# Last three projection tiles and part of the first row tile's projection placed among the first 45 attention units; sample transfers reordered

## The reference

```
z = h @ w_in                                   # q, k, v are the last three blocks of 256 columns
q, k = rms(q, q_norm) * 64**-0.5, rms(k, k_norm)
for win, dil in ((128,1), (512,4), (2048,16)): # prompt: blocks of 128 queries, 256 keys;
    s = q @ k.T + bias; m = max(s); p = exp(s - m); o = p @ v / sum(p)   # samples: + 2048 cached rows
attn = softmax-weighted merge of the patterns' outputs
mix = concat(out_a, out_b, out_c, attn), each of the four normalized
x  = x + g1 * (mix @ w_out)
h2 = rms(x) * (1 + sc2) + sh2
x  = x + g2 * moe(h2)                          # 4 groups x 8 experts, two per token
```

## Time and profile before

| | us |
|---|---|
| median of 3 runs | 2401.43 |
| the runs | 2401.43, 2389.86, 2404.76 |
| profiled execution | 2399.02 |
| its span, first to last instruction | 2397.3 |
| PE busy / DVE / ACT / POOL | 2175.1 / 853.0 / 562.8 / 284.5 |
| mean granted clock | 0.944 |
| DMA | 438.91 MB, mean 183 GB/s |

### The profile page before, as it was taken

How to read it: one execution, slowest core, us unless ns; L and a number is a source line. 1 busy time by engine, 2 the same in 40 slices (tenths; PEclk the granted TensorE clock), 3 DMA queues, 4 the chain that set the end, 5 groups by cost and what they waited for, 6 DMA issues and landing times.

```text
span 2397.3 us, 27992 instructions
## 1 busy us (share of the span) xinstructions
PE 2175.1 (91%) x7615; PEld 1094.5 (46%) x7616; DVE 853.0 (36%) x1969; ACT 562.8 (23%) x1110; POOL 284.5 (12%) x463
## 2 busy tenths in 40 slices
PE   4999999999797999999598199999999999999895
PEld 1344455545454755656234144444444444444342
DVE  3566464026562455564464511111111111111112
ACT  3410010235532434443122111111111111111111
POOL 0001020100000000001131211111111111111111
PEclk8999999999898589999899599999999999999998
DMA  9253132433447522234754545765479788787873
GB/s 377 94 215 84 31 84 51 158 105 97 126 142 204 174 76 100 87 107 152 237 204 177 190 148 161 269 229 157 162 271 344 261 325 299 238 287 290 293 248 71
DMA packets 122756, 438.91 MB, mean 183 GB/s; under 512 B 31955, under 2 KB 70579, under 8 KB 102115
## 3 DMA queue, kind: packets, MB, share of 16 engines
q1 hardware_dynamic: 92520, 309.99, 35.3%
q0 software_dynamic: 26032, 112.64, 17.2%
q10 hardware_dynamic: 4112, 15.14, 1.6%
HBM read 356.39 MB, written 83.10 MB: 183 GB/s over the span
## 4 chain that ended last, share of the span: by engine, by line
PE 81%; DVE 6%; DMA 5%; issue 3%; ACT 2%; POOL 1%; SPq 1%; DVEq 0%; ACTq 0%; POOLq 0%
PE bank L2550 20%; PE bank L2191 15%; PE bank L2578 10%; PE bank L2455 7%; PE bank L2554 4%; PE bank L2299 3%; PE bank L2354 3%; PE bank L2331 2%; PE bank L2581 2%; PE bank L2516 2%; PE bank L2341 2%; PE bank L2303 1%; PE bank L2271 1%; DMA arena<-xT 1%; DMA arena<-kc 1%
## 5 line engine op out<-in xcount | busy, mean ns | idle before, releaser
L2550 PE MATMUL bank<-arena 128*128 128x512 f32 x1120 | 492.8, 596 | 14.7 <-issue 14.7
L2191 PE MATMUL bank<-arena 128*128 128x512 f32 (+1 forms) x960 | 358.2, 533 | 9.6 <-ACTq L1066 9.6
L2550 PEld LDWEIGHTS bank<-arena 128*128 128x128 f32 x1120 | 212.6, 191 | 290.9 <-issue 290.9
L2578 PE MATMUL bank<-arena 128*128 128x512 f32 x560 | 249.6, 598 | 12.8 <-issue 12.6
L2191 PEld LDWEIGHTS bank<-arena 128*128 128x128 f32 x960 | 168.0, 191 | 193.6 <-issue 192.8
L2455 PE MATMUL bank<-arena 128*128 128x512 f32 x512 | 245.8, 604 | 0.0
L2083 DVE COPY arena<-bank 128x512 f32<-128x512 f32 x50 | 34.7, 693 | 552.0 <-PE bank L2565 552.0
L2578 PEld LDWEIGHTS bank<-arena 128*128 128x128 f32 x560 | 103.0, 189 | 136.5 <-issue 128.7
L2093 DVE TENSOR_TENSOR arena<-bank,arena 128x512 f32<-128x512 f32 (+1 forms) x50 | 34.5, 691 | 257.0 <-PE bank L2578 212.1
L2455 PEld LDWEIGHTS bank<-arena 128*128 128x128 f32 x512 | 88.6, 192 | 77.1 <-issue 77.0
L985 POOL DMA_INDIRECT o_y<-arena x50 | 79.3, 1585 | 310.5 <-issue 172.8
(11 more groups left out here) (475 smaller groups left out, 2564.6 us busy)
## 6 DMA issues: line engine op xcount, KB each, us to landing
arena<-wg SPq DMA_DIRECT2D x32, 2048.0 KB, 12.1
arena<-wu SPq DMA_DIRECT2D x32, 2048.0 KB, 16.9
arena<-wd SPq DMA_DIRECT2D x32, 2048.0 KB, 8.1
arena<-mod_w SPq DMA_DIRECT2D x12, 2048.0 KB, 18.2
z_d<-arena ACTq DMA_DIRECT2D x12, 1056.0 KB, 6.5
arena<-z_d POOLq DMA_DIRECT2D x10, 1056.0 KB, 7.7
arena<-kc POOLq DMA_DIRECT2D x8, 1280.0 KB, 10.6
arena<-vc POOLq DMA_DIRECT2D x8, 1280.0 KB, 8.2
```

The source lines that it names most:

```text
L2191: ins = mm(bank[n % 2][:, 0:w], wz[:, i % 3, k, :], hT[:, k, t0:t0 + w], start=(k == 0), stop=(k == KT - 1))
L2550: ins = mm(bank[bk][:, :], xgT[:, s, k, :], m[w][:, k, :], start=(k == 0), stop=(k == KT - 1))
L2578: ins = mm(bank[4 + h][:, :], hhT[:, k, :], wd[w][:, k, 512 * h:512 * h + 512], start=(k == 0), stop=(k == 3))
```

## The change

The list of steps is changed:

```diff
-                    ("outBn",), *tile(12), *tile(13), ("ldq", 0), *tile(14), ("ldq", 1), ("t1p",), *tile(15), ("ldq", 2), *tile(16), *tile(17), *tile(18),
-                    ("ldq", 4), ("smp",)]
+                    ("outBn",), *tile(12), ("ldq", 0), ("qkv", 13), ("qkn", 12), ("qkl", 11), ("ql", 14, 0), ("qkn", 13), ("ql", 14, 1), ("t1p",),
+                    ("ql", 14, 2), ("qe", 14), ("qkl", 12), ("smp",)]
+        BESIDE = {0: [("qkn", 14)], 2: [("qkl", 13)], 4: [("ql", 15, 0)], 6: [("ldq", 1)], 8: [("ql", 15, 1)], 12: [("ql", 15, 2), ("qe", 15)],
+                  13: [("qkn", 15)], 14: [("ldq", 2)], 15: [("qkl", 14)], 17: [("ql", 16, 0)], 21: [("ql", 16, 1), ("qe", 16)], 22: [("qkn", 16)],
+                  24: [("qkl", 15)], 26: [("qkl", 16), ("ldq", 4)], 28: [("ldq", 3)], 30: [("mx", 0)], 48: [("qb",)]}
+        for n in range(6):
+            BESIDE[34 + 2 * n] = [("p", 0, *divmod(n, 3))]
...
-        for f, hf, first in (("sS", 0, (4, 9)), ("sS", 1, (18, 25)), ("sV", 0, (17, 22)), ("sV", 1, (33, 38))):
+        for f, hf, first in (("sS", 0, (0, 8)), ("sS", 1, (17, 24)), ("sV", 0, (16, 21)), ("sV", 1, (32, 37))):
...
-        for hf, b, t, o in ((0, 10, 14, 25), (1, 26, 30, 41)):
+        for hf, b, t, o in ((0, 9, 13, 24), (1, 25, 29, 40)):
...
-        for n, f, bs in ((-4, "kc", (0, 1)), (1, "ts", ()), (1, "vc", (0, 1, 2)), (7, "kc", (2, 3)), (12, "kc", (4, 5)), (20, "vc", (3, 4)),
-                         (21, "kc", (6, 7)), (25, "vc", (5, 6)), (36, "vc", (7,))):
+        for n, f, bs in ((-4, "kc", (0, 1)), (0, "ts", ()), (3, "kc", (2, 3)), (4, "vc", (0, 1, 2)), (11, "kc", (4, 5)), (19, "vc", (3, 4)),
+                         (20, "kc", (6, 7)), (24, "vc", (5, 6)), (35, "vc", (7,))):
...
-            out = [("qb",)] if u == 4 else [("ldq", 3)] if u == 28 else []
+            out = BESIDE.get(u, [])
...
-            out = [("p", i, j // 4, j % 4)] + out
+            early = [("mx", 0), *(("p", 0, q, part) for q in range(2) for part in range(3))]
+            out = [s for s in [("p", i, j // 4, j % 4)] + out if s not in early]
```

"ql" is a tile's projection in three parts on PE (two halves of the queries and keys, into bank 5, then the values; tile 16 in two parts of both side by side), "qe" the rest of "qkv" on ACT and DVE, "qkl" the transposes into bank 6 with the same copies and stores. A part of 4 steps of k is 8 matmuls:

```diff
+            def qkv_late(step, i, part):
+                r, t0 = rows(i), i * P
+                ks = range(4 * part, 4 * part + 4) if part < 2 else range(KT)
+                if part == 0:
+                    if i == LATE:
+                        mx_left(pe, 2)
+                    else:
+                        pe.wait_ge(S("qk_ready"), i)
...
+                if part == 2:
+                    pe.wait_ge(S("v_free"), i)
+                for k in ks:
+                    if part < 2:
+                        mm(bank[5][:, :], hT[:, k, t0:t0 + r], wqkv[:, k, 0:512], start=(k == 0), stop=(k == KT - 1))
+                    else:
+                        ins = mm(bank[7][:, 0:256], hT[:, k, t0:t0 + r], wqkv[:, k, 512:768], start=(k == 0), stop=(k == KT - 1))
+                if part == 2:
+                    ins.then_inc(S("v_mm"), 1)
...
+            def qkt_late(step, i):
+                r = rows(i)
+                pe.wait_ge(S("qk_ready"), i + 1)
+                if i == 11:
+                    mx_left(pe, 3)
+                else:
+                    pe.wait_ge(S("qkT_ready"), i)
+                for q in range(4):
+                    ins = pe.transpose(bank[6][:, q * P:q * P + r], qks[0:r, i % 3, q * P:(q + 1) * P], ident[0:r, 0:r])
+                ins.then_inc(S("late_turned"), 1)
```

The attention's tiles keep off the columns of hT that tiles 15 and 16 still need: pt is shifted by 64 for u < 32, and two of the output tiles, the small constant eps_c and the default table move to other places. On POOL:

```diff
             def smp(step):
                 pool.wait_ge(S("st_mix"), 16 * 16)
+                pool.wait_ge(S("v_mm"), NT)
+                pool.dma_start(wo, A["w_out"]).then_inc(S("ld_wo"), 16)
...
-                pool.wait_ge(S("v_mm"), NT)
-                pool.wait_ge(S("att_o"), AT["att_o"] + 1)
-                pool.dma_start(wo, A["w_out"]).then_inc(S("ld_wo"), 16)
-                pool.wait_ge(S("att_o"), AT["att_o"] + 3)
                 pool.dma_start(nrow, A["nffn"].broadcast_to([P, D])).then_inc(S("ld_rows"), 16)
+                link(pool.memset(dflt, 0))
+                link(pool.iota(dflt[:, :, 1], pattern=[[0, NBLK - 1]], base=T, channel_multiplier=1))
+                pool.dma_start(tok_v[:, 0:NBLK - 1, :], dflt).then_inc(S("st_dflt"), 16)
+                pool.dma_start(tok_v[:, NBLK - 1:NBLK, :], dflt[:, 0:1, :]).then_inc(S("st_dflt"), 16)
+                pool.wait_ge(S("st_dflt"), 32)
...
                     else:
                         pool.wait_ge(S("att_pv"), AT["att_pv"] + NU)
                         pool.wait_ge(S("att_max"), AT["att_max"] + NU)
+                        for q in range(2):
+                            pool.wait_ge(S(f"ld_kc{q}"), 32)
```

More of the change, by code:

```diff
@@ L296, in build @@
         modrow = take(2 * 512, v_at).rearrange("p (n m) -> p n m", n=2)
-        eps_c = sm[:, 399:400]
+        eps_c = take(1, 53199)
         def stage_a(j):
@@ L431, in build, with qk_bank @@
         RING = sum(TILES.get(s[0], 0) for s in SCHEDULE)
+        LATE = 14
+        def qk_bank(i):
+            return bank[i % 3][:, :] if i < LATE else bank[5][:, :]
         def mx_left(pe, q):
@@ L481, in keys, with turned_at @@
             return x[:, :, BK * k:BK * b + BK].rearrange("p r (b m) -> p b r m", m=BK)
+        def turned_at(u):
+            return T - 2048 if u < 32 else 0
         def att_rows(block):
@@ L655, in smp_out, with sample_bias @@
                 sp.dma_start(smp_d[4 * hf:4 * hf + 4].rearrange("b h s c -> (b h s) c"), so).then_inc(S("st_smp"), 16)
+            def sample_bias(step, bs):
+                sp.wait_ge(S("att_pT"), AT["att_pT"] + NU)
+                sp.wait_ge(S("att_pv"), AT["att_pv"] + NU)
+                sp.wait_ge(S("st_v0"), 16 * 9)
+                for b in range(4):
+                    for h in range(4):
+                        p0 = 32 * b + 8 * h
+                        sp.dma_start(ts[p0:p0 + 8, :], bass.AP(tensor=sk3_d.tensor, offset=h * 8 * L3 + 7,
+                                                                 ap=[[L3 - 1, 8], [1, 2056]])).then_inc(S("ld_ts"), 16)
+                sp.dma_start(hsel, A["hsel"]).then_inc(S("ld_ts"), 16)
             def row_att(step, i):
@@ L1182, in qkv @@
                     act.wait_ge(S("qk_ss"), i - 1)
[L1183 removed]
+                link(act.activation(ksq[i % 2][0:r], qk_bank(i)[0:r], ACT.Square))
                 act.sem_inc(S("qk_sq"), 1)
@@ L1199, in qkt @@
             def qkt(step, i):
-                r = rows(i)
-                n = base[step]
-                act.wait_ge(S("mx_full"), n + 1)
+                late = step[0] == "qkl"
+                if late:
+                    act.wait_ge(S("late_turned"), i - 10)
+                    b = bank[6][:, :]
+                else:
+                    n = base[step]
+                    act.wait_ge(S("mx_full"), n + 1)
+                    b = mx(n)
                 if i:
@@ L2328, in att_scores @@
                     pe.wait_ge(S(f"ld_q{c}"), 16 * 7)
-                if u >= 2:
+                if u < 2:
+                    pe.wait_ge(S("qk_ready"), 13 + u)
+                else:
                     pe.wait_ge(S("att_max"), AT["att_max"] + u - 1)
```

62 lines of the change are left out of this document (32 added, 30 removed).

## The result

| | before | after |
|---|---|---|
| median of 15 runs each, us | 2395.44 | 2383.83 |
| the runs | 2389.21 to 2405.94 | 2378.08 to 2388.94 |
| profiled execution, us | 2399.02 | 2388.94 |
| its span | 2397.3 | 2387.2 |
| mean granted clock | 0.944 | 0.952 |

The ratio of the runs is 0.9943, with a 95% interval from 0.9932 to 0.9954: 13.7 us faster (the medians are 11.6 apart). The forecast was 34 us. The time is inside the stated range, but the gain is 0.4 of what I forecast, and under the 1% that I gave 0.72 to. The profiled execution after, 2388.94, is the slowest of its fifteen.

What follows compares the result with a forecast made beforehand. The prediction took TensorE to bound the kernel, busy nearly throughout, with half clock in attention and a 23.2 us key stall. From 2399, 8 us off beside attention and 26 off the sample transfers gave 2365, range 2340 to 2388.

Steps and rivals of the forecast that it cites:

- Part A: Projections and six row parts moved beside attention, 731.55 to 878.20 us: 138 against 146.65, 8 us less.
- units 4 to 21: Attention with the dense projections of tiles 15 and 16: five bursts, six wide and three narrow pairs, chains; 48 us.
- units 22 to 33: Attention without dense work at half clock, with 2 us for the stores of turned tiles; 17 us.
- 2 at unit 34 for its operands: Wait for output weights and mixed rows at the first moved row part: 2 us, bounds 0 and 23.
- The queue paragraph: SP's chunk loads move, stores of turned tiles stand behind them; chunk 0's landing and the default table's store are hidden.
- F: Attention with no idle gap holds the full clock: projections beside attention 27 us less, total 2346; chance 0.20.
- P: Short row parts don't lift the clock: projections beside attention 13 us more, total 2386; chance 0.20.
- Part B: Sample transfers, 1126 to 1210 us: keys 2 and 3 asked for ahead of values; 26 us less, bounds 14 and 32.
- median landing 10.6: Keys 2 and 3 land at the median 10.6 us, near 1146, so unit 140 waits 0 to 3 us.
- rival K: Key stall only shrinks, the DMA being shared with the rows' traffic: half stays, 14 us less, 2377; chance 0.08.
- The slow side: In-order engines wait on stores and mixed rows: 46 us more than counted, 2411, deciding from 35 us; chance 0.04.
- the likeliest case: 8 us less beside attention and 26 less in the sample transfers: 34 less, 2365; chance 0.48.

## Why the prediction was wrong

**Part A**, term by term, from the scores' rows of the two traces. Of the 17.8 us by which the traces fall short of the forecast 34, A accounts for 13.1 and B for 4.7. The changed kernel has the wait for the mixed rows, the kernel with chunk 3 later has 0.6 us left at unit 34:

| | forecast | changed | chunk 3 later |
|---|---|---|---|
| tile 14 | 10.8 | 10.9 | 10.9 |
| units 0 to 3 | 7.3 | 6.5 | 6.5 |
| units 4 to 21 | 48 | 43.6 | 43.5 |
| units 22 to 33 | 17 | 21.5 | 22.0 |
| units 34 to 49 | 33 | 46.5 | 32.5 |
| units 50 to 57, to unit 58's part | 22 | 22.8 | 22.7 |
| sum | 138 | 151.8 | 138.1 |

The step that failed is "2 at unit 34 for its operands": 13.3. I had its bounds right (0 and 23) and the reason too, "behind chunk 3's keys and values", and then took a value near the lower end, by the minimum and median in the earlier trace rows. But the 23.3 there is of the request at 1141.46 us, among the samples' loads, and the first mixed rows, behind a chunk, are like that one; those asked for before it had landed within 4.8. The value should have gone by the landing with the same company. The gain that I had forecast for A was there to be had: with the mixed rows first and chunk 3 later A is 8.6 us shorter, where I had said 8. That the figures agree so closely is in part luck, as the next terms show.

The queue paragraph failed in a second way. I named the stores of turned tiles as what stands behind the chunk loads, and not the stores of the attention's outputs, whose three tiles hold up VectorE, and through it the maxima. That was worth 4.1 us once the first wait was gone, 10.5 with the parts back.

Two terms were wrong and cancelled. Units 4 to 21 came 4.4 us cheaper, which I have not split between clock and chains. Units 22 to 33 came 4.5 dearer: ScalarE's wait for a store (4.07 us, for which I had 2 in all) at half clock with VectorE's small waits.

**The clock** behaved as said, and the rivals about it fell. F, that attention holds it: 0.52 in 862 to 872 of the changed kernel, 0.55 in the 34 us of 812 to 846 with the parts back. The Trainium skill (TensorE: Matmul & The Clock Gate, section on why this matters for your kernels) would have had the clock full wherever TensorE had no gaps. These stretches have gaps, but others have none: in the kernel before, TensorE was busy 60.00 of 60 us from 778 to 838 with the clock at half throughout, and with the parts back 17.00 of 17. Both speak against that rule, as the row under L2321 in the earlier trace rows does. Before, then parts back:

```profile
778.00:838.00 60.00, 60.00 (x264) 47.74 (x262) 28.16 (x117) 28.88 (x103) 3.54 (x8) 0.50 0.56 175
```

```profile
815.00:832.00 17.00, 17.00 (x75) 13.28 (x74) 7.48 (x29) 8.11 (x27) 3.43 (x6) 0.50 0.77 258
```

P, that short parts don't lift it: the part after unit 34's took 1.88 us in every version that has the parts there. P's time (2386) is near the measured one for another reason, and only the trace tells the two apart.

**Moving the parts.** I wrote that the sum "wins little" on them. No gain shows: the ratios are 0.9888 and 0.9882 with some 4 us of interval each way, and the stretch takes 54.2 us moved and 54.9 left. The prices of my own sum had it so: 33 + 22 with the parts moved against 29.6 + 24.4 with them left. I should have drawn the conclusion that the move brings a risk (operands 16 units sooner) for no gain.

**Part B** was forecast at 26 and is 21.3 in the trace, 19.9 in the runs of the part alone. The stall was to go less 1.5 us; 6.3 are left, and the half clock behind it is as before (3.63 and 2.99 us). The failing step is "median landing 10.6": the second of keys 2 and 3 landed 18.0 us after its issue, and TensorE went on 18.7 us after the request (1141.90 to 1160.56). Counted from unit 132, the request came when I had said (8.8 us behind it, forecast 9), and so did TensorE to unit 140 (21.5, forecast 21.6). The median was of keys that had the DMA mostly to themselves. The ones asked for in unit 135 share it with the stores of a row tile and its loads, which I left out (I had only "1 MB of bias ahead"). That is rival K in part: the wait shrank and did not go. The values' wait on ScalarE went altogether, 6.7 rather than 3, and 5.8 came up at the transposes of normalized rows: the bound that I gave ("a late DVE stays late for something") in another place. The Trainium skill (Trainium Kernel Development and Optimization, Key Constraints) says that DMAs issued from SP, ACT and POOL all run on the same 16 DMA engines. In the kernel with the slices cut, keys from POOL's queue and rows' transfers from SP's together kept the DMA 0.99 busy from 1127 to 1144, which agrees. It bears on the size of B and not just on which queue issues the slices.

**The slow side** was the right mechanism: an in-order queue with a transfer at its head. It needed 35 us in sum to decide and had 17: 13.3 for the mixed rows, and 4.07 at one of the four stores. With 0.04 for it and nothing between it and the likeliest case I had no case for "one of these waits, at its measured length", which is what came.

What stays open: why the kernel with the later second pair took some 10 us longer in 12 of its 13 executions than in the first. Its second trace shows where (the load of the rows' attention), not why only at times.

## What to carry to other kernels

A step that is moved takes its transfers along: for each, find the row of a landing with the same loads ahead of it, and take that one, not the median. Where several waits lie at one place, taking one away shows the next, so list all that the same queue holds (loads wanted, stores that free a buffer) before pricing. When the DMA is full over a stretch, reordering within it moves the wait from one consumer to another, as three versions here did (the second pair later, the slices copied, the gate rows later); that fewer bytes there would shorten it is argued, since the one version that had them (the slices copied) gained no time. Ask also what is counted on the same semaphore as the operand that you price. And a dense burst laid beside light work paid for itself here at the full clock without bringing time: price both placements in full before moving work to an earlier place with tighter operands.

## What the runs showed of the hardware that I had not expected

A key load of 1.3 MB landed 10.6 us after its issue at the median of the kernel before, and 18.0 when a row tile's transfers went with it. The experts' stretch, with one code, took 999.4 to 1006.2 us over 17 traces, so a single profile does not resolve less than about 7 us of the whole kernel. The interval A resolves more: A was 373.9 to 376.5 us in five kernels with the same edits there (chunk 3 later, and four on top of it that change only what comes later or is hidden). B does not: it was 256.5 to 262.3 us in nine kernels with the samples' steps as changed, and 262.9 and 270.5 in two traces of one kernel, so a few us of B from one trace prove nothing by themselves.
